# Two more slots for expert weights, and another order at three places of the linear attention

## What is computed

```python
def gla_mixer(x, w_in, gate_w, gate_b, norm_g, w_out):
    q, k, v, r, glr = jnp.split(x @ w_in, [...], axis=-1)
    loga = log_sigmoid(einsum('bsgr,grk->bsgk', glr, gate_w) + gate_b) / GLA_TAU   # two directions
    o = gla_chunked(q, k, v, loga[fwd]) + flip(gla_chunked(flip(q), ..., flip(loga[bwd])))
    return (silu(r) * head_norm(o, norm_g)) @ w_out

def ec_moe(x, w_router, w_gate, w_up, w_down):
    aff = softmax(x @ w_router)
    gates, idx = lax.top_k(swapaxes(aff, 1, 2), 32)
    xin = x[bidx, idx]
    h = silu(einsum('becd,edf->becf', xin, w_gate)) * einsum('becd,edf->becf', xin, w_up)
    out = einsum('becf,efd->becd', h, w_down) * gates[..., None]
    return zeros_like(x).at[bidx, idx].add(out)
```

## Time and profile before

| | us |
|---|---|
| median of 3 runs (1741.91 to 1742.19) | 1742.12 |
| profiled execution | 1742.07 |
| its span | 1740.0 |
| TensorE busy (80% of the span) | 1396.3 |
| VectorE busy (34%) | 594.0 |
| ACT busy (25%) | 428.8 |
| DMA: bytes moved | 533.71 MB, mean 307 GB/s |
| granted TensorE clock, mean | 0.906 of full |

### The profile page before, as it was taken

The page is one execution under the profiler, slowest core; times in us unless marked ns, Lnnn a source line. Parts: engine busy times, 40 slices in busy tenths (PEclk is TensorE's granted clock), DMA queues, the critical chain, the costliest instruction groups (busy, mean ns, idle before and its releaser), DMA issues.

```text
span 1740.0 us, 21541 instructions
## 1 busy us (share of the span) xinstructions
PE 1396.3 (80%) x9022; PEld 915.9 (53%) x9022; DVE 594.0 (34%) x993; ACT 428.8 (25%) x700; POOL 41.9 (2%) x53
## 2 busy tenths in 40 slices
PE   8999576575665999995655656559999999999997
PEld 8786121121211675751211212116999989899996
DVE  5663000010000357630000100004555566865556
ACT  3552000000000333420000000002434455654343
POOL 3000000000000012000000000000000000000000
PEclk9999787787788999997887878879999999999999
DMA  9858999999999943689999999999465764245550
GB/s 326 255 213 338 424 423 424 423 423 424 424 424 424 381 150 125 243 351 424 424 424 422 424 424 424 424 424 349 145 194 176 247 206 144 74 135 180 193 193 24
DMA packets 149030, 533.71 MB, mean 307 GB/s; under 512 B 9964, under 2 KB 73724, under 8 KB 100700
## 3 DMA queue, kind: packets, MB, share of 16 engines
q1 hardware_dynamic: 145088, 527.01, 77.3%
q10 hardware_dynamic: 2236, 2.25, 0.7%
q0 software_dynamic: 1632, 3.38, 0.6%
HBM read 529.98 MB, written 2.62 MB: 306 GB/s over the span
## 4 chain that ended last, share of the span: by engine, by line
PE 38%; DMA 19%; DVE 3%; SPq 3%; ACT 1%; issue 0%; DVEq 0%; ACTq 0%
PE bank L1827 15%; PE bank L1843 7%; PE bank L693 5%; DMA moe_slots<-in_moe_w_up 4%; DMA ring<-in_moe_w_up 4%; DMA arena<-in_moe_w_up 3%; DMA arena<-in_moe_w_down 3%; PE bank L532 3%; DMA ring<-in_moe_w_down 2%; PE bank L1233 2%; SPq L1427 2%; DMA xT<-in_moe_w_down 1%; PE bank L1273 1%; PE bank L313 1%; PE bank L1518 1%; DVE stats L340 1%
## 5 line engine op out<-in xcount | busy, mean ns | idle before, releaser
L612 DVE TENSOR_TENSOR w_lo<-ring,w_hi 128x1024 fp32r<-128x1024 f32 x187 | 228.6, 1224 | 191.9 <-ACT w_hi L607 191.6
L607 ACT ACTIVATE w_hi<-ring 128x1024 fp32r<-128x1024 f32 x187 | 197.8, 1059 | 260.6 <-PE bank L1827 150.3
L1233 PE MATMUL bank<-ring,arena 128*32 128x512 f32 x1024 | 153.7, 729 | 81.7 <-DMA ring<-in_moe_w_up 81.6
L1827 PE MATMUL bank<-xT_hi,w_hi 128*128 128x256 f32 x704 | 199.9, 284 | 0.5 <-DVE xT_lo L495 0.3
L1827 PE MATMUL bank<-xT_lo,w_hi 128*128 128x256 f32 x704 | 199.4, 283 | 0.0
L1827 PE MATMUL bank<-xT_hi,w_lo 128*128 128x256 f32 x704 | 199.4, 283 | 0.0
L1273 PE MATMUL bank<-ring,arena 128*32 128x512 f32 x544 | 131.5, 799 | 81.8 <-DMA ring<-in_moe_w_down 36.2
L1392 DVE TENSOR_TENSOR arena<-arena,bank 64x512 f32<-64x512 f32 x32 | 22.1, 691 | 433.1 <-ACT arena L1328 433.1
L1827 PEld LDWEIGHTS bank<-xT_hi,w_hi 128*128 128x128 f32 x704 | 135.2, 192 | 1.5 <-issue 0.8
L1827 PEld LDWEIGHTS bank<-xT_lo,w_hi 128*128 128x128 f32 x704 | 135.2, 192 | 0.7
L1827 PEld LDWEIGHTS bank<-xT_hi,w_lo 128*128 128x128 f32 x704 | 135.2, 192 | 0.0
(11 more groups left out here) (293 smaller groups left out, 2294.0 us busy)
## 6 DMA issues: line engine op xcount, KB each, us to landing
ring<-in_moe_w_gate SPq DMA_DIRECT2D x64, 1024.0 KB, 26.7
ring<-in_moe_w_up SPq DMA_DIRECT2D x64, 1024.0 KB, 26.4
ring<-in_moe_w_down SPq DMA_DIRECT2D x64, 1024.0 KB, 26.9
arena<-in_moe_w_gate SPq DMA_DIRECT2D x28, 1024.0 KB, 26.7
arena<-in_moe_w_up SPq DMA_DIRECT2D x28, 1024.0 KB, 26.6
moe_slots<-in_moe_w_up SPq DMA_DIRECT2D x24, 1024.0 KB, 26.4
moe_slots<-in_moe_w_gate SPq DMA_DIRECT2D x24, 1024.0 KB, 26.7
moe_slots<-in_moe_w_down SPq DMA_DIRECT2D x24, 1024.0 KB, 26.9
```

The costliest lines, as they stand in the source:

```text
L607: nc.scalar.activation(dst, raw, ACT.Copy).then_inc(hi_ready, 1)
L612: nc.vector.tensor_tensor(lo, raw, hi.bitcast(F32), ALU.subtract).then_inc(split_ready, 1)
L1233: last = nc.tensor.matmul(ps[B_GU[j % 2]][32 * c:32 * c + 32, :], xin[:, k, j * CAP:(j + 1) * CAP], w, start=(k == 0), stop=(k == KD - 1), ...
L1827: last = nc.tensor.matmul(ps[2 * s + f][:, n * SEQ:(n + 1) * SEQ], w_parts[wp][:, buf, k * P:(k + 1) * P], (xT_hi3, xT_lo3)[xp][:, k, :], ...
```

## The change

`NSLOT` is 22. Slot 20 (`SPARE_SLOT`) lies in `arena` from column 2816, slot 21 (`CONST_SLOT`) is made of the two pieces `cst[:, 256:1280]` and `gk_w`, and is loaded in two halves of 0.5 MB. To make room in the arena, silu's tile goes, and `hT` shares its columns with `xin`, whose layout becomes expert by expert. The last 22 units of a layer don't use the constants' slot. The gate weights are loaded by GpSimd after that slot's last use in layer 0. The four semaphores of the tail become one. In linear attention level 0 goes to banks 6 and 7 like level 7, VectorE's `q_side(0)` and `args(1)` come before the copies of the diagonal, and the first silu pair is taken after level 5's exponentials. `gla_mix.hi(act, 0)` comes ahead of `ln_scalar(act, 1)`, and the warm-up is 7 products instead of 12.

```diff
-NSLOT = 20
+NSLOT = 22
+SPARE_SLOT, CONST_SLOT = 20, 21
...
-        self.landed[s] += 16
+        self.landed[s] += 32 if s == CONST_SLOT else 16
...
-        for slots, u in ((ARENA_SLOTS, mixer[11]), (SPLIT_SLOTS, mixer[15]), ((XT_SLOT,), mixer[15])):
+        for slots, u in (((CONST_SLOT,), mixer[8]), ((*ARENA_SLOTS, SPARE_SLOT), mixer[11]), (SPLIT_SLOTS, mixer[15]), ((XT_SLOT,), mixer[15])):
...
-        return self.units(count, range(NSLOT))
+        return self.units(count - NSLOT, range(NSLOT)) + self.units(NSLOT, range(CONST_SLOT))
...
+        spare_at = 2816
+        slots += [arena[:, spare_at:spare_at + SLOT], None]
+        const_rows = (cst[:, C_SEL:C_SEL + D], gk_w[:, :])
...
-        xin = ar(KD * SLOTS_E).rearrange("p (k c) -> p k c", k=KD)
-        silu = ar(2 * HALF).rearrange("p (b n) -> p b n", b=2)
+        xin_hT = ar(KD * SLOTS_E)
+        xin = xin_hT.rearrange("p (j k c) -> p j k c", j=GROUP, k=KD)
+        hT = xin_hT.rearrange("p (b c) -> p b c", b=2)
         hmid = ar(2 * HALF).rearrange("p (b n) -> p b n", b=2)
...
-                    for landed in tail_landed:
-                        pe.wait_ge(landed, 16 * (m + 1))
+                    pe.wait_ge(tail_landed, 16 * GROUP * (m + 1))
...
                     act.wait_ge(unit_done, us[8 * j + 7].done_at())
-                    nc.scalar.activation(silu[64:128, j % 2, :], ps[B_GU[j % 2]][0:64, :], ACT.Silu).then_inc(silu_ready, 1)
+                    if j == 0 and g:
+                        act.wait_ge(scattered, n - m)
+                    elif j % 2:
+                        act.wait_ge(h_ready, 4 * n + j)
+                    nc.scalar.activation(hmid[64:128, j // 2, :], ps[B_GU[j % 2]][0:64, :], ACT.Silu).then_inc(silu_ready, 1)
...
+                elif u.slot == CONST_SLOT and m == 0:
+                    sp.wait_ge(const_ready, 2)
+                    sp.wait_ge(chunk_done, ml_mix.done(15))
+                elif u.slot == CONST_SLOT:
+                    sp.wait_ge(ga_psum, 1)
+                elif u.slot in ARENA_SLOTS or u.slot == SPARE_SLOT:
                     sp.wait_ge(z_ready[1], m + 1)
...
+            def load(u, src):
+                if u.slot == CONST_SLOT:
+                    for k in range(2):
+                        sp.dma_start(const_rows[k], src[:, k * D:(k + 1) * D]).then_inc(slot_landed[u.slot], 16)
+                else:
+                    sp.dma_start(slots[u.slot], src).then_inc(slot_landed[u.slot], 16)
...
-        level_bank = lambda n, i: i if n < len(LEVELS) - 1 else 6 + i
+        level_bank = lambda n, i: i if 0 < n < len(LEVELS) - 1 else 6 + i
...
-            keep_clock(5, 12)
+            keep_clock(5, 7)
...
             pe.wait_ge(glr_ready, 1)
+            pe.wait_ge(gk_in, 8 * 16)
...
                 m, i = n // 2, n % 2
+                if n == 2:
+                    pe.wait_ge(lv_done, 2)
...
-                if n == 0:
-                    pe.wait_ge(diag_ready, 2)
-                elif level_bank(n, 0) == 0:
+                if 0 < n < len(LEVELS) - 1:
                     pe.wait_ge(lv_done, 2 * n)
-                else:
+                elif n:
                     pe.wait_ge(gv_ready, 4)
...
-                for m in {1: (0,), 3: (1,), 7: (2, 3)}.get(n, ()):
+                if n % 2:
+                    m = n // 2
                     act.wait_ge(unit_done, gla_u[5 + 2 * m].done_at())
...
             args(0)
+            q_side(0)
+            args(1)
             dve.wait_ge(diag_psum, 1)
             for i in range(NT):
                 nc.vector.tensor_scalar(gl_A[:, i, :, i * P:(i + 1) * P], ps[i][:, :].rearrange("p (h t) -> p h t", h=4),
                                         2.0, None, ALU.mult).then_inc(diag_ready, 1)
-            q_side(0)
-            args(1)
...
-        MISC = 16 * 11
+        MISC = 16 * 3
...
+        def gk_gpsimd(pool, link):
+
+            pool.wait_ge(unit_done, max(u.n for u in moe_u[0] if u.slot == CONST_SLOT) + 1)
             link(nc.gpsimd.memset(gk_w[:, :], 0.0))
             for q in range(4):
                 for d in range(2):
                     at = (2 * q + d) * RANK
-                    pool.dma_start(gk_w[at:at + RANK, d * QK:(d + 1) * QK], a["gla_gate_w"][0, d]).then_inc(misc_in, 16)
+                    pool.dma_start(gk_w[at:at + RANK, d * QK:(d + 1) * QK], a["gla_gate_w"][0, d]).then_inc(gk_in, 16)
...
+            gla_mix.hi(act, 0)
             ln_scalar(act, 1)
-            gla_mix.hi(act, 0)
             xT_scalar(act, 2)
...
             ml_gpsimd(pool)
+            gk_gpsimd(pool, link)
             gla_gpsimd(pool)
```

More of the change, by code:

```diff
@@ L235, in program, with slot_row @@
         slots += [moe_slots[:, n * SLOT:(n + 1) * SLOT] for n in range(4)] + [xT[:, :]]
+        spare_at = 2816
+        slots += [arena[:, spare_at:spare_at + SLOT], None]
+        const_rows = (cst[:, C_SEL:C_SEL + D], gk_w[:, :])
+        def slot_row(u, k):
+            return const_rows[k] if u.slot == CONST_SLOT else slots[u.slot][:, k * D:(k + 1) * D]
         def slot(u, k):
@@ L1143, in program @@
         pick_gT = ar(NT * P)
-        assert ar.at <= arena_w - 4 * SLOT
+        assert ar.at <= spare_at and spare_at + SLOT <= arena_w - 4 * SLOT
         ar = Arena()
@@ L1158, in program @@
         pick_ready, pickg_ready, gathered = (sem(s) for s in ("pick_ready", "pickg_ready", "gathered"))
-        tail_landed = [sem(f"tail{j}_landed") for j in range(GROUP)]
+        tail_landed = sem("tail_landed")
         xin_act, xin_vec, pickT_psum, pickT_ready = (sem(s) for s in ("xin_act", "xin_vec", "pickT_psum", "pickT_ready"))
@@ L1231, in gate_up @@
                             for c in range(4):
-                                w = slot((ug, uu)[c // 2], 2)[:, k2, (c % 2) * HALF:(c % 2 + 1) * HALF]
+                                w = slot_row((ug, uu)[c // 2], k2)[:, (c % 2) * HALF:(c % 2 + 1) * HALF]
                                 last = nc.tensor.matmul(ps[B_GU[j % 2]][32 * c:32 * c + 32, :],
-                                                        xin[:, k, j * CAP:(j + 1) * CAP], w, start=(k == 0),
+                                                        xin[:, j, k, :], w, start=(k == 0),
                                                         stop=(k == KD - 1), tile_position=(0, 32 * c))
@@ L1322, in moe_scalar @@
                     for k in (2 * part, 2 * part + 1):
-                        ins = nc.scalar.activation(xin[:, k, :], xin_psum(k), ACT.Identity,
+                        ins = nc.scalar.activation(xin[:, :, k, :], xin_psum(k).rearrange("p (j c) -> p j c", j=GROUP), ACT.Identity,
                                                    bias=pair_col(m, 1, k), scale=pair_col(m, 0, k))
@@ L1389, in moe_vector @@
                     dve.wait_ge(silu_ready, 4 * n + j + 1)
-                    if j == 0 and g:
-                        dve.wait_ge(scattered, n - m)
-                    nc.vector.tensor_tensor(hmid[64 * (j % 2):64 * (j % 2) + 64, j // 2, :], silu[64:128, j % 2, :],
+                    nc.vector.tensor_tensor(hmid[64 * (j % 2):64 * (j % 2) + 64, j // 2, :], hmid[64:128, j // 2, :],
                                             ps[B_GU[j % 2]][64:128, :], ALU.mult).then_inc(h_ready, 1)
@@ L1418, in moe_sync @@
                             src = a[name][m, g * GROUP + j].rearrange("(q p k) f -> p q (k f)", p=P, k=2)
-                            sp.dma_start(slots[u.slot], src[:, part, :]).then_inc(slot_landed[u.slot], 16)
+                            load(u, src[:, part, :])
                 for q in range(KD // 2):
@@ L1425, in moe_sync @@
                         src = a["moe_w_down"][m, g * GROUP + j].rearrange("(q p k) d -> p q k d", p=P, k=2)
-                        cols = slice(0, HALF if tail else D)
-                        sp.dma_start(slot(u, 2)[:, :, cols], src[:, q, :, cols]).then_inc(slot_landed[u.slot], 16)
+                        if tail:
+                            sp.dma_start(slot(u, 2)[:, :, 0:HALF], src[:, q, :, 0:HALF]).then_inc(slot_landed[u.slot], 16)
+                        else:
+                            load(u, src[:, q].rearrange("p k d -> p (k d)"))
                     if tail:
@@ L1430, in moe_sync @@
                             src = a["moe_w_down"][m, g * GROUP + j].rearrange("(q p k) d -> p q k d", p=P, k=2)
-                            sp.dma_start(slot(us[44 + j], 2)[:, :, HALF:D], src[:, q, :, HALF:D]).then_inc(tail_landed[j], 16)
+                            sp.dma_start(slot(us[44 + j], 2)[:, :, HALF:D], src[:, q, :, HALF:D]).then_inc(tail_landed, 16)
         ar = Arena()
```

9 lines of the change are left out of this document (3 added, 6 removed).

## The result

The changed kernel takes 1738.38 us (median; 1735.19 to 1741.11), the kernel before beside it 1742.37 us (1741.73 to 1745.12): a ratio of 0.9976, 95% interval 0.9970 to 0.9983, so 4.0 us faster where 8.25 were forecast. The profiled execution took 1737.63 us with a span of 1735.3.

A forecast was written before the change was run, and what follows sets the result against it. Expert stages are bound by weight loads on full DMA, the rest by a TensorE chain. Terms -9.9 + 0.6 + 0 + 0.1 - 4.45 + 3.5 + 1.9 = -8.25 from 1742.07 give 1733.8 us; range 1727.5 to 1739.0.

The forecast's parts named there:

- Level 7: Linear attention, silu moved to level 5: TensorE waits 3.5 us for level 7's queries, then 1.9 us of low clock.
- Rival (a): Linear attention: the new wait at level 7 is missing, so 1728.4 us; chance 0.12.
- (b): At level 7: the wait is cheaper, no table load or no fall of the clock, 1730.6 to 1732.5 us; chance 0.13.
- (c): ACT's table switch ahead of level 7: it has a drain beside the load, so 1735.2 us; chance 0.05.
- Level 0: Linear attention: queries first and banks 6 and 7 remove a 2.56 us wait and 1.89 us of low clock, -4.45 us.
- The split: First split ahead of the norm: the square root waits for ACT, +0.1 us (-0.5 to +0.6).
- rival (e): SP's queue: each issue holds it 2.1 us however small, so the kernel is slower, 1761.5 us; chance 0.04.
- the 1.5 that was named as a sign of being wrong: SP's queue: the prediction is wrong if half loads hold SP over 1.5 us.
- My step "nothing is added": Constants' slot: its two 0.5 MB issues hold SP 1.19 us each, half of a whole load's 2.5, so no cost.
- Gate weights: First expert stage: the eight moved loads are hidden on POOL but ride in the plateau, +0.6 us (0 to 1).
- Slots: Expert stages: two more slots per layer land 2 MB before the refill, 4 x 2.473 = -9.9 us.

The follow-up runs named there:

- Experiment 1: The changed kernel with the silu of the first gate half back behind level 7's exponentials: 1732.75 us for the changed kernel's 1738.4.
- experiment 9: The changed kernel with the first split behind the square root again and 12 warm-up products: 1735.47 us, one execution.
- experiments 6: The kernel of experiment 5 with the fourth load of each refill split into two loads of 1024 columns: 1737.5 us.
- kernel of 7: The kernel of Experiment 1 with the constants' slot last instead of first in the cycle of the 22 slots: 1731.05 us.
- experiment 2: The changed kernel without the eight gate weight loads, so the decay gates are computed from zeros: 1734.71 us.
- Experiment 3: The kernel of Experiment 1 with the eight gate weight loads issued on SP's queue instead of POOL's: 1734.28 us.
- experiment 4: The kernel before with 72 expert loads in two halves: of 1024 columns, 1745.29 us; of 64 partitions, four executions of 1946, 1974, 1993 and 2039 us.
- experiment 5: The kernel before with the spare slot alone (21 slots, arena packed as in the change, no constants' slot): 1735.67 us.

## Why the prediction was half right

The direction was right and the time lies in the range, but the gain was half the forecast. What failed are two terms: the price of the gate weights' loads, and that of the constants' slot's half loads, which was put at nothing. By the steps, with the profiled executions (4.4 us gained for 8.25):

- **Level 7** was right in mechanism and size: a wait of 3.7 us for 3.5, 1.13 + 0.79 = 1.9 us of low clock for 1.9. Experiment 1 gives 5.6 for 5.4 together. Rival (a) is out. So is the first half of (b), no table load; its second half, a wait without a fall of the clock, is what the trace of experiment 9 shows, so the 1.9 isn't there each time. (c) is out as well: the table load ran 678.23 to 679.51 and Exp at 679.52, 1.29 us with no drain beside it. The Trainium skill ("ScalarE: Activation LUTs", "What ACT_TABLE_LOAD costs") gives a switch a drain of 1.38 us beside the load; the trace disagrees.
- **Level 0** was right: the wait is gone, 16 products in 1.79 us. In the trace of after all of its 2.56 + 1.27 + 0.62 us are gone. Alone it brought 3.9 us in the medians for 4.45. That the clock makes the rest is likely and not shown: in the same place it fell in one trace and not in another.
- **The split** was right within 0.2 us (+0.2 or nothing for +0.1), and ACT did become what the square root waits for.
- **SP and the half loads**: rival (e) was right that a half can hold SP 2.1 us, and wrong that it costs: SP makes it up, 0.04 us a load. The halves hold SP 2.12 and 2.10 us in after as well (the slot's loads at 197 us), over the 1.5 that was named as a sign of being wrong, and the sign was a bad one. My step "nothing is added" took the row of 1.19 us, and was wrong in another way: at the start of a refill the halves lose 0.7 to 1.0 us of DMA rate, once a layer (experiments 6 and 7). No row of before has a load in halves in such a queue. It was a term without bounds, which it should have had. The Trainium skill ("DMA: Bandwidth & Descriptors", "Bandwidth") says to batch to 1 MiB or more; the runs bear it out as the fourth load of a refill (341 GB/s for 426), and not for the full queue, where halves of 0.5 MB keep 422 GB/s.
- **Gate weights** were mis-sized: +0.6 (0 to 1) for a measured 2.5 (experiment 2: 2.6 of stage 0). I counted their bytes at the plateau's rate, which is the rate of loads of 1 MB to all 128 partitions. In the trace their own packets take 1.0 us, and the experts' packets beside them lose another 1.5. Experiment 3 shows that the queue isn't the reason, experiment 4 that loads to 64 partitions halve the rate.
- **Slots**: -9.9 for two slots in two layers. One loaded whole brought 2 x 2.4 (experiment 5). The constants' slot, with its dip and some 0.3 us for eight loads in halves a layer, brought 1.3 in the second layer. The kernel of 7 reaches 4.4 of 4.95 there.

In stage 0 the gate weights (2.0), the dip (1.0) and the later halves (0.3) make 3.3 us, and 431.7 - 428.4 = 3.3 were missing. In stage 1 the dip (0.7) and the halves (0.3) make 1.0 of 1.4; the last 0.4 stays open. Equal programs differ by up to 0.5 us here, so neither that rest nor the exact agreement in stage 0 says much.

The refill's start and the router's products gave 0.6 and 1.0 us that no term had. Without them the profiled execution would have gained 2.8 us and taken 1739.3, just above the range. So the forecast missed by more than the time shows, and that the time lies in the range is in part luck.

## What to carry to other kernels

Count what rides in a full DMA stream by what it does to the rate, not by its bytes: loads to a part of the partitions belong where the DMA engines have time to spare, and a buffer gained by moving them into the plateau can cost what it brings. Read the price from a row in which such a load stands beside full ones, and if there is none, give the term bounds. A new slot that has to be loaded in pieces should come up when the queue is deep, not first in a refill. And when a helper engine's work is moved ahead of a queue's next step, sum up the distance to the last consumer in that queue, as was done for level 7: that number held to 0.2 us.

## What the hardware showed unexpectedly

- Loads of 1 MB as two of 64 partitions: 338 GB/s over 100 us at a DMA share of 1.02, and 210 to 246 where they are under way, where two of 1024 columns keep 422. Eight loads of 32 KB to 16 partitions: 2.5 us for 0.6 by bytes, on either queue, 1.5 of it by slower packets of the loads beside them.
- After the same idle time of TensorE (2.56 us, 3.7 us) the granted clock fell to 0.63 to 0.82 in one trace and stayed 1.00 in that of another kernel with the same wait. The first mixer shows the same without any difference in the program there and without idle time: the kernel before, then the kernel of 5, which starts its refill 2.5 us later. It loses 1.6 of them between 60 and 64 us, and 0.8 ahead of 30 us, where both clocks read 1.00.

```profile
60.00:80.00 20.00, 20.00 (x90) 16.56 (x89) 13.83 (x29) 10.41 (x13) 1.85 (x4) 1.00 0.77 212
```
```profile
60.00:80.00 20.00, 20.00 (x82) 16.35 (x82) 14.61 (x32) 11.18 (x13) 1.86 (x4) 0.92 0.73 195
```

  Every other kernel started that refill near 155 or near 158 us. Each kernel has one trace, so whether this goes by the execution or by the kernel isn't shown; that the times of the kernel of 5 lie in two groups 2.7 us apart speaks for the execution. A time read from one execution of this kernel can then be off by 2 us and more. The stage lengths begin behind it, and equal programs agree in them within 0.5 us.
